# GpSimd in place of VectorE for the two adds of product P1 in the down projection of a one-layer encoder

## The chip, the core and the metric

One core of a Trainium2 chip runs the whole program. TensorE (PE in the rows) multiplies, VectorE (DVE), ScalarE (ACT) and GpSimd (POOL) do the elementwise work, SyncE (SP) issues most DMAs. Each engine takes its own instructions in order and waits on semaphores. The metric is the device time of one execution in microseconds (us), lower is better.

## The reference, cut to what matters

One layer: a forgetting attention and then a dense SwiGLU, each on a normalised residual stream, in float32. S = 512 rows, D = 2048, D_FF = 5632.

```python
h = rmsnorm(x, mix_norm_g[i])
x = x + forgetting_attention(h, fox_w_in[j], ...)
h = rmsnorm(x, ffn_norm_g[i])
x = x + swiglu(h, ffn_w_gate_up[i], ffn_w_down[i])

def swiglu(h, w_gu, w_down):
    gu = jnp.einsum('bsd,df->bsf', h, w_gu)
    gate, up = gu[..., :D_FF], gu[..., D_FF:]
    return jnp.einsum('bsf,fd->bsd', jax.nn.silu(gate) * up, w_down)
```

Only the second product, `w_down`, with the sum into x, is touched here: "down" in what follows.

## The kernel before, in words

**Numbers in two parts.** Each float32 operand is split into a high part (rounded, ScalarE) and a low part (the rest, VectorE), and each product is three matmuls: high by high, high by low, low by high. For a weight tile, `weights_hi` (L1007, L1010, L1014) on ScalarE writes `f_hi`, and `weights_lo` (L1344) on VectorE subtracts it from `f_raw` to get `f_lo`. For the hidden activations, `down_forms_lo` (L1414) does the same on VectorE.

**Seven products in place of eight.** The SwiGLU runs Strassen's scheme in Winograd's form on 2 x 2 blocks. So the work is in units: one unit is one slice of weights with three products (first half of a round, g = 0: P1, P2 and P3) or four (second half, g = 1: P5, P6, P7 and P4). A unit with g = 0 has 18 matmuls of 128 x 512 and one with g = 1 has 24. For g = 1, VectorE first makes sums of the raw weights in place: `sums_t1_t3` (L1350) and `sums_t2_t4` (L1355, L1357); ScalarE and then `weights_lo` follow on these. PE takes a unit when its `f_lo` is done. In PE's rows a unit begins where the output changes from `gemm` to `aux` at L723.

**Rounds.** A round is ROUND_K units with g = 0 and then as many with g = 1. Rounds 0 to 10 are gate and up, rounds 11 to 16 are down: three blocks of 8, 7 and 7 steps, with two rounds each. Around the first round of a block the activations' forms are loaded, so L1414 stands between the weight operations there.

**The results.** In down the results are summed into the tile `rows`, which holds x1, the residual stream. It was stored to DRAM (`dram_x1`, "x_scratch" in the rows) and comes back with four DMAs on SP's queue: `rows[:, 2]` (L390) and `rows[:, 0]` (L393) in round 11, `rows[:, 1]` (L396) and `rows[:, 3]` (L397) right behind the weight loads of the third unit of round 12, that is when PE is done with the last unit but one of round 11. For each of the two column pairs n, GpSimd makes a base of them, an add (L510) and a subtract (L512), when both DMAs of the pair have landed. Even n belongs to rounds 11, 13, 15, odd n to rounds 12, 14, 16.

**At the end of the first half** of a down round r, ScalarE copies the two banks of P1 to `junk_act` (L1027, semaphore `p1_read`), and VectorE adds P2 (L1423, `p2_read`) and P3 (L1428, `p3_read`; in rounds 11 and 12 after GpSimd's base, `base_done`) from PSUM into `rows`. `add_p1`, of which the change is, then adds P1 into two blocks of `rows`: `x1 += P1` (L1436, semaphore `x1_p12`) and `x4 = P1 - x4` (L1437, `x4_p1`), both 128 x 1024 from SBUF to SBUF. VectorE reaches it at unit j = 4 of the second half.

**At the end of the second half**, `down_read` on VectorE waits for `x4_p1` and reads P6 (L1445, `p6_read`) and P7 (L1450 and L1451, `p7_read`) from PSUM, `add_p4` (L1458) reads P4, and at the start of the next round `add_p5` (L1467) and `finish_x4` (L1482) follow. PE may overwrite the banks of P1 in the next round only after `p6_read`. ScalarE's next copy into `junk_act` waits for `x4_p1`.

**Order.** It is written out by hand, per engine, by loops over the units; there is no planner.

Of the kernel before, what the change touches and what calls it, by code (L numbers as in the profile page):

```python
# [30 lines left out]
ALU = mybir.AluOpType  # L31
# [7 lines left out]
def encoder_layer(nc, x, mix_g, ffn_g, w_in, b_f, g_q, g_k, w_out, w_gu, w_down, y):  # L39
# [33 lines left out]
    R_DOWN = NP  # L73
    NR = NP + 2 * len(BLOCKS)
# [20 lines left out]
    with ctx:  # L95
        def at(name, offset, shape, dt=F32):
            return nc.alloc_sbuf_tensor_at(name, shape, dt, offset=offset)

        def sem(name):
            return ctx.enter_context(nc.semaphore(name))  # L100
# [41 lines left out]
        rows = at("rows", AREA_S, [P, ND, NT, CW])  # L142
# [10 lines left out]
        def small(name, shape, dt=F32):  # L153
            n = 4
            for s in shape[1:]:
                n *= s
            offset = place[0]
            place[0] += -(-n // 32) * 32
            assert place[0] <= 229344
            return at(name, offset, shape, dt)  # L160

        junk_act = small("junk_act", [P, 2, CW])
# [24 lines left out]
        def a_lo(k):  # L187
# [47 lines left out]
        p1_read, p2_read, p3_read = sem("p1_read"), sem("p2_read"), sem("p3_read")  # L235
        p6_read, p5_read, p7_read, p4_read = (sem("p6_read"), sem("p5_read"),
                                              sem("p7_read"), sem("p4_read"))
# [8 lines left out]
        x1_p12, x4_p1, x2_p5, x4_p7 = sem("x1_p12"), sem("x4_p1"), sem("x2_p5"), sem("x4_p7")  # L246
# [28 lines left out]
        for b in range(len(BLOCKS)):  # L275
            r = R_DOWN - 1 + 2 * b
# [145 lines left out]
        def _(pool):  # L422
            g = nc.gpsimd
# [83 lines left out]
            for n in range(2):  # L507
                pool.wait_ge(x1_ld[n], 16)
                pool.wait_ge(x1_ld[2 + n], 16)
                g.tensor_tensor(rows[:, n, 2:4], rows[:, n, 2:4], rows[:, 2 + n, 2:4], ALU.add)\  # L510
                    .then_inc(base_done, 1)
                g.tensor_tensor(rows[:, 2 + n, 0:2], rows[:, 2 + n, 0:2], rows[:, 2 + n, 2:4],  # L512
                                ALU.subtract).then_inc(base_done, 1)


        @block.tensor
# [594 lines left out]
        def _(dve):  # L1111
            v = nc.vector
# [23 lines left out]
            def row_sums(n):  # L1136

                dve.wait_ge(ssx_done, NT * ND * (n + 1))
                v.tensor_reduce(ss_sum[:], ss_x[:], AX.X, ALU.add).then_inc(sum_done, 1)
# [148 lines left out]
            def form_sums(q, fa):  # L1288
                dve.wait_ge(xform_read, 2 * q + 2)
                block_sums(q, fa)  # L1290

            def form_lo(q, fa):
                dve.wait_ge(aform_hi, q + 1)
                v.tensor_tensor(a_form[:, q, 1], fa[:, 0:7], f32(a_form[:, q, 0]), ALU.subtract)\
                    .then_inc(aform_lo, 1)
# [45 lines left out]
            def weights_lo(n):  # L1341
                g = UNITS[n][1]
                dve.wait_ge(f_hi_done, HI_COUNT[n])
                v.tensor_tensor(f_lo[:, n % 4, 0:3 + g], f_raw[:, n % 4, 0:3 + g],  # L1344
                                f32(f_hi[:, n % 3, 0:3 + g]), ALU.subtract).then_inc(f_lo_done, 1)

            def sums_t1_t3(n):
                dve.wait_ge(f_ld[n % 4], LANDED[n])
                f = f_raw[:, n % 4]
                v.tensor_tensor(f[:, 0:2], f[:, 0:2], f[:, 1:4:2], ALU.add).then_inc(t_step, 1)  # L1350

            def sums_t2_t4(n):
                f = f_raw[:, n % 4]
                dve.wait_ge(t_step, 3 * T_COUNT[n] + 1)
                v.tensor_tensor(f[:, 3], f[:, 0], f[:, 3], ALU.add).then_inc(t_step, 1)  # L1355
                dve.wait_ge(t_step, 3 * T_COUNT[n] + 2)
                v.tensor_tensor(f[:, 2], f[:, 3], f[:, 2], ALU.add).then_inc(t_step, 1)  # L1357
# [28 lines left out]
            def up_top(r):  # L1386
                for t in range(2):
                    dve.wait_ge(p3_read, 2 * r + t + 1)
                    dve.wait_ge(p5_read, 2 * r + t + 1)
                    v.tensor_tensor(h_top[:, t], h_top[:, t], h_bot[:, t], ALU.add).then_inc(c12_done, 1)  # L1390
# [37 lines left out]
                    v.tensor_tensor(rows[:, 2 + n, t], bank_c[t][:], rows[:, 2 + n, t], ALU.add)\  # L1428
                        .then_inc(p3_read, 1)

            def add_p1(r):
                n = (r - R_DOWN) % 2
                dve.wait_ge(p1_read, 2 * r + 2)
                dve.wait_ge(p2_read, 2 * r + 2)
                x1, x4 = rows[:, n, 0:2], rows[:, 2 + n, 2:4]
                v.tensor_tensor(x1, x1, junk_act[:], ALU.add).then_inc(x1_p12, 1)  # L1436
                v.tensor_tensor(x4, junk_act[:], x4, ALU.subtract).then_inc(x4_p1, 1)  # L1437

            def down_read(r):
                n = (r - R_DOWN) % 2  # L1440
                dve.wait_ge(x4_p1, r - R_DOWN + 1)
                for t in range(2):
                    wait_product(dve, r, True, t)
                    x4 = rows[:, 2 + n, 2 + t]
                    v.tensor_tensor(x4, bank_a[t][:], x4, ALU.add).then_inc(p6_read, 1)  # L1445
                for t in range(2):
                    dve.wait_ge(p6_read, 2 * r + t + 1)
                    wait_product(dve, r, True, 4 + t)
                    x4, x3 = rows[:, 2 + n, 2 + t], rows[:, 2 + n, t]
                    v.tensor_tensor(x4, bank_b[t][:], x4, ALU.add).then_inc(x4_p7, 1)  # L1450
                    v.tensor_tensor(x3, bank_b[t][:], x3, ALU.add).then_inc(p7_read, 1)  # L1451
# [49 lines left out]
            for n in range(NU):  # L1501
                r, g, j = UNITS[n]
                hidden = 1 <= r <= R_DOWN
                last = j == ROUND_K[r] - 1
                sums = n + 2 < NU and UNITS[n + 2][1] == 1
                meeting = (g == 0 and j == ROUND_K[r] - 2) or (g == 1 and j == 0)
                if sums and not meeting:
                    sums_t1_t3(n + 2)
                if n + 1 < NU:
                    weights_lo(n + 1)  # L1510
                if sums and meeting:
                    sums_t1_t3(n + 2)
                if sums:
                    sums_t2_t4(n + 2)
                if g == 0:
                    if r == 0:
                        if j == 1:
                            form_sums(6, fa_a)
                        if j == 2:
                            form_lo(6, fa_a)  # L1520
                            form_sums(7, fa_b)
                        if j == 3:
                            form_lo(7, fa_b)
                            row_sums(1)
                    if hidden:
                        if j == 0:
                            up_top(r - 1)
                        if j == 1:
                            hidden_top(r - 1)
                        if j == 2:  # L1530
                            hidden_bot(r - 1)
                        if j == 3:
                            hidden_sums(r, 0)
                        if j == 5:
                            hidden_sums(r, 1)
                    if r > R_DOWN:
                        if j == 0:
                            add_p5(r - 1)
                            finish_x4(r - 1)
                        if r == NR - 1 and j == 1:  # L1540
                            last_sums(r - 1)
                        if r == NR - 1 and j == 2:
                            last_bottom(r - 1)
                    if last:
                        if r < R_DOWN:
                            read_p2(r)
                        else:
                            add_p2_p3(r)
                else:
                    if r >= R_DOWN and j == 4:  # L1550
                        add_p1(r)
                    if last and r < R_DOWN:
                        second_pass_read(r)
                    if last and r >= R_DOWN:
                        down_read(r)
                        if r < NR - 1:
                            add_p4(r)
                        else:
                            add_p5(r)
                            finish_x4(r)  # L1560
                            last_sums(r)
                            last_bottom(r)
                            add_last_p4(r)
                if n - 4 in LOAD_AT:
                    down_forms_lo(*LOAD_AT[n - 4])
# [24 lines left out]
```

## Time and profile before

| what | us |
|---|---|
| time, median of 3 runs | 2190.46 |
| lowest and highest of the 3 | 2188.57, 2190.71 |
| the profiled execution's own time | 2189.52 |
| its span in the trace | 2187.8 |
| around the span | 1.7 |

In the page PE is busy for 97% of the span, DVE for 70%, ACT for 42%, POOL for 8%. In the 40 slices DVE is at 4 to 5 tenths in the attention and at 7 to 9 tenths from slice 16 on, in the SwiGLU. Down takes about the last fifth of the span. A row of the time line reads: start, duration, engine, line, operation, output<-inputs, shape, count of merged instructions, and in brackets the idle time of the engine ahead of it with what ended it.

### The profile page before, as it was taken

The numbers are of one execution on the slowest core, as the hardware profiler recorded it, in microseconds if no ns is written. First come the engines' busy times: TensorE is split into PE (matmuls) and PEld (weight loads), VectorE is DVE, ScalarE is ACT, GpSimd is POOL, SyncE is SP. The second block draws the span as 40 slices with busy tenths as digits, with TensorE's granted clock in tenths as the row PEclk, the third lists the DMA queues.
The fourth block names the chain that finished last, engine by engine and source line by source line (L and its number), as shares of the span: only waits on it lengthen the run. The fifth ranks groups of instructions, "written<-read, shape, count | busy, mean of one in ns | idle before, by whom it ended". The sixth has DMA issues, their size and how long they took to land.

```text
span 2187.8 us, 27845 instructions
## 1 busy us (share of the span) xinstructions
PE 2129.5 (97%) x10404; PEld 1852.7 (85%) x10404; DVE 1524.6 (70%) x2103; ACT 915.4 (42%) x1225; POOL 183.8 (8%) x356
## 2 busy tenths in 40 slices
PE   9999999999999999999999999999999989999997
PEld 8999999999998887888888888888887777777786
DVE  4544444444464445987888888788798888898888
ACT  5433333333343334444444444444445534444432
POOL 0322213222230000000000000000000001000000
PEclk9999999999999999999999999999999999999999
DMA  6332333333343335566566566567668757757755
GB/s 181 88 92 82 88 85 90 85 89 81 92 144 135 116 106 163 178 226 220 179 222 226 177 219 229 190 207 228 193 207 280 261 201 270 236 177 250 234 175 178
DMA packets 258331, 376.30 MB, mean 172 GB/s; under 512 B 15762, under 2 KB 114100, under 8 KB 257220
## 3 DMA queue, kind: packets, MB, share of 16 engines
q1 hardware_dynamic: 254864, 354.90, 51.6%
q10 hardware_dynamic: 3380, 20.21, 2.2%
q8 instruction: 58, 0.95, 0.2%
q14 instruction: 29, 0.24, 0.0%
HBM read 346.45 MB, written 28.61 MB: 171 GB/s over the span
## 4 chain that ended last, share of the span: by engine, by line
PE 83%; DVE 9%; DMA 6%; issue 1%; SPq 1%; POOL 0%; ACT 0%; DVEq 0%; POOLq 0%; ACTq 0%
PE gemm L522 11%; PE gemm L524 11%; PE gemm L523 11%; PE gemm L723 8%; PE gemm L725 8%; PE gemm L724 8%; PE aux L723 7%; PE aux L725 7%; PE aux L724 6%; DVE f_lo L1344 4%; DMA f_raw<-in_ffn_w_gate_up 3%; DMA f_raw<-in_ffn_w_down 2%; DVE f_raw L1350 2%; PE aux L523 1%; PE aux L524 1%; PE aux L522 1%
## 5 line engine op out<-in xcount | busy, mean ns | idle before, releaser
L1344 DVE TENSOR_TENSOR f_lo<-f_raw,f_hi 128x2048 fp32r<-128x2048 f32 (+1 forms) x264 | 534.2, 2030 | 63.9 <-ACT f_hi L1007 51.4
L522 PE MATMUL gemm<-w_hi,act_t 128*128 128x384 f32 (+2 forms) x1280 | 450.6, 352 | 1.6 <-DVE w_lo L1123 1.6
L524 PE MATMUL gemm<-w_hi,act_t 128*128 128x384 f32 (+2 forms) x1280 | 444.0, 347 | 0.0
L523 PE MATMUL gemm<-w_lo,act_t 128*128 128x384 f32 (+2 forms) x1280 | 443.9, 347 | 0.0
L723 PE MATMUL gemm<-f_hi,a_form 128*128 128x512 f32 x1056 | 412.4, 391 | 0.4 <-DVE rows L1428 0.4
L724 PE MATMUL gemm<-f_lo,a_form 128*128 128x512 f32 x1056 | 411.7, 390 | 0.0
L725 PE MATMUL gemm<-f_hi,a_form 128*128 128x512 f32 x1056 | 411.3, 389 | 0.0
L723 PE MATMUL aux<-f_hi,a_form 128*128 128x512 f32 x792 | 318.3, 402 | 42.8 <-DVE f_lo L1344 42.8
L725 PE MATMUL aux<-f_hi,a_form 128*128 128x512 f32 x792 | 312.2, 394 | 0.0
L724 PE MATMUL aux<-f_lo,a_form 128*128 128x512 f32 x792 | 311.9, 394 | 0.0
L1123 DVE TENSOR_TENSOR w_lo<-w_raw,w_hi 128x768 fp32r<-128x768 f32 (+1 forms) x160 | 160.8, 1009 | 208.5 <-ACT w_hi L818 208.5
L1007 ACT ACTIVATE f_hi<-f_raw 128x1536 fp32r<-128x1536 f32 x132 | 196.0, 1487 | 253.8 <-PE gemm L725 93.2
L522 PEld LDWEIGHTS gemm<-w_hi,act_t 128*128 128x128 f32 x1280 | 241.0, 188 | 12.4 <-issue 2.0
L523 PEld LDWEIGHTS gemm<-w_lo,act_t 128*128 128x128 f32 x1280 | 241.0, 188 | 10.4
L524 PEld LDWEIGHTS gemm<-w_hi,act_t 128*128 128x128 f32 x1280 | 240.8, 188 | 10.1
L723 PEld LDWEIGHTS gemm<-f_hi,a_form 128*128 128x128 f32 x1056 | 199.1, 189 | 42.6 <-DVE rows L1428 0.8
L724 PEld LDWEIGHTS gemm<-f_lo,a_form 128*128 128x128 f32 x1056 | 199.0, 188 | 41.6
L725 PEld LDWEIGHTS gemm<-f_hi,a_form 128*128 128x128 f32 x1056 | 198.8, 188 | 41.7
L1010 ACT ACTIVATE f_hi<-f_raw 128x1024 fp32r<-128x1024 f32 x132 | 139.9, 1060 | 222.2 <-DVE f_raw L1350 218.2
L1014 ACT ACTIVATE f_hi<-f_raw 128x1024 fp32r<-128x1024 f32 x132 | 140.2, 1062 | 210.5 <-DVE f_raw L1357 210.5
L723 PEld LDWEIGHTS aux<-f_hi,a_form 128*128 128x128 f32 x792 | 150.3, 190 | 88.2 <-DVE f_lo L1344 58.5
L818 ACT ACTIVATE w_hi<-w_raw 128x768 fp32r<-128x768 f32 (+1 forms) x160 | 136.4, 883 | 187.8 <-PE gemm L524 187.8
(161 smaller groups left out, 2143.0 us busy)
## 6 DMA issues: line engine op xcount, KB each, us to landing
f_raw<-in_ffn_w_gate_up SPq DMA_DIRECT2D x264, 512.0 KB, 4.2
f_raw<-in_ffn_w_down SPq DMA_DIRECT2D x132, 512.0 KB, 4.8
w_raw<-in_fox_w_in SPq DMA_DIRECT2D x192, 256.0 KB, 3.4
f_raw<-in_ffn_w_gate_up SPq DMA_DIRECT2D x88, 256.0 KB, 4.0
w_raw<-in_fox_w_out SPq DMA_DIRECT2D x16, 1024.0 KB, 5.1
a_raw<-forms_scratch SPq DMA_DIRECT2D x22, 512.0 KB, 6.3
f_raw<-in_ffn_w_down SPq DMA_DIRECT2D x44, 256.0 KB, 4.8
forms_scratch<-fa_a ACTq DMA_DIRECT2D x11, 896.0 KB, 6.3
```

Source lines behind the costliest of these rows:

```text
L522: mm(out, a_hi, b_hi, start=first, stop=False)
L523: mm(out, a_hi, b_lo, start=False, stop=False)
L524: return mm(out, a_lo, b_hi, start=False, stop=last)
L723: mm(banks[t][:], st_hi, hi, start=j == 0, stop=False)
L724: mm(banks[t][:], st_hi, lo, start=False, stop=False)
L725: i = mm(banks[t][:], st_lo, hi, start=False, stop=j == ROUND_K[r] - 1)
L818: a.activation(w_hi[:, j % 2, k, 0:width], w_raw[:, j % 2, k, 0:width], ACT.Copy)\
L1007: a.activation(f_hi[:, n % 3, 0:3], f_raw[:, n % 4, 0:3], ACT.Copy).then_inc(f_hi_done, 1)
L1010: a.activation(f_hi[:, n % 3, 0:2], f_raw[:, n % 4, 0:2], ACT.Copy).then_inc(f_hi_done, 1)
L1014: a.activation(f_hi[:, n % 3, 2:4], f_raw[:, n % 4, 2:4], ACT.Copy).then_inc(f_hi_done, 1)
L1123: v.tensor_tensor(w_lo[:, j % 2, k, 0:width], w_raw[:, j % 2, k, 0:width], f32(w_hi[:, j % 2, k, 0:width]), ALU.subtract).then_inc(w_lo_do ...
L1344: v.tensor_tensor(f_lo[:, n % 4, 0:3 + g], f_raw[:, n % 4, 0:3 + g], f32(f_hi[:, n % 3, 0:3 + g]), ALU.subtract).then_inc(f_lo_done, 1)
```

## The change

The two adds leave VectorE's list and stand at the end of GpSimd's, one pair for each of the six down rounds, with the same semaphores. GpSimd waits for `p1_read` and `p2_read` of the round, does the first add, waits for `p5_read` of the round before (VectorE's last subtract into x4), and does the second.

```diff
@@ gpsimd, behind the two base operations of each n
+            for r in range(R_DOWN, NR):
+                n = (r - R_DOWN) % 2
+                pool.wait_ge(p1_read, 2 * r + 2)
+                pool.wait_ge(p2_read, 2 * r + 2)
+                x1, x4 = rows[:, n, 0:2], rows[:, 2 + n, 2:4]
+                g.tensor_tensor(x1, x1, junk_act[:], ALU.add).then_inc(x1_p12, 1)
+                pool.wait_ge(p5_read, 2 * (r - 1))
+                g.tensor_tensor(x4, junk_act[:], x4, ALU.subtract).then_inc(x4_p1, 1)
@@ vector
-            def add_p1(r):
-                n = (r - R_DOWN) % 2
-                dve.wait_ge(p1_read, 2 * r + 2)
-                dve.wait_ge(p2_read, 2 * r + 2)
-                x1, x4 = rows[:, n, 0:2], rows[:, 2 + n, 2:4]
-                v.tensor_tensor(x1, x1, junk_act[:], ALU.add).then_inc(x1_p12, 1)
-                v.tensor_tensor(x4, junk_act[:], x4, ALU.subtract).then_inc(x4_p1, 1)
@@
                 else:
-                    if r >= R_DOWN and j == 4:
-                        add_p1(r)
                     if last and r < R_DOWN:
```

**GpSimd's list, its end.** Before, the last compute instructions are the two base pairs of n = 0 and n = 1 (the numbers behind the names tell tiles apart):

```order
95 L505 TENSOR_SCALAR rms_neg_98<-rms_x_97 128x4 [waits rms_done]
96 L510 TENSOR_TENSOR rows_82<-rows_82 128x1024 [waits x1_loaded2,x1_loaded0]
97 L512 TENSOR_TENSOR rows_82<-rows_82 128x1024
98 L510 TENSOR_TENSOR rows_82<-rows_82 128x1024 [waits x1_loaded3,x1_loaded1]
99 L512 TENSOR_TENSOR rows_82<-rows_82 128x1024
100 L95 UNCONDITIONAL_BRANCH
```

With the change (L520 and L522 are the two adds of P1; rounds 13 to 16 repeat the last two rows):

```order
96 L510 TENSOR_TENSOR rows_82<-rows_82 128x1024 [waits x1_loaded2,x1_loaded0]
97 L512 TENSOR_TENSOR rows_82<-rows_82 128x1024
98 L510 TENSOR_TENSOR rows_82<-rows_82 128x1024 [waits x1_loaded3,x1_loaded1]
99 L512 TENSOR_TENSOR rows_82<-rows_82 128x1024
100 L520 TENSOR_TENSOR rows_82<-rows_82,junk_act_90 128x1024 [waits p2_read,p1_read]
101 L522 TENSOR_TENSOR rows_82<-junk_act_90,rows_82 128x1024 [waits p5_read]
102 L520 TENSOR_TENSOR rows_82<-rows_82,junk_act_90 128x1024 [waits p2_read,p1_read]
103 L522 TENSOR_TENSOR rows_82<-junk_act_90,rows_82 128x1024 [waits p5_read]
```

The pair of round 11 (100 and 101) stands behind the base of n = 1, which waits for the two loads that are issued in the last unit of round 11.

**VectorE's list, second half of round 11.** Before, from unit j = 4 to the reads of P6 and P7:

```order
1036 L1357 TENSOR_TENSOR f_raw<-f_raw 128x512 [waits t_step]
1037 L1436 TENSOR_TENSOR rows<-rows,junk_act 128x1024 [waits p2_read,p1_read]
1038 L1437 TENSOR_TENSOR rows<-junk_act,rows 128x1024
1039 L1350 TENSOR_TENSOR f_raw<-f_raw 128x1024 [waits f_loaded3]
1040 L1344 TENSOR_TENSOR f_lo<-f_raw,f_hi 128x2048 [waits f_hi_done]
1041 L1355 TENSOR_TENSOR f_raw<-f_raw 128x512 [waits t_step]
1042 L1357 TENSOR_TENSOR f_raw<-f_raw 128x512 [waits t_step]
1043 L1344 TENSOR_TENSOR f_lo<-f_raw,f_hi 128x2048 [waits f_hi_done]
1044 L1344 TENSOR_TENSOR f_lo<-f_raw,f_hi 128x1536 [waits f_hi_done]
1045 L1445 TENSOR_TENSOR rows<-aux,rows 128x512 [waits product_done,x4_p1]
1046 L1445 TENSOR_TENSOR rows<-aux,rows 128x512 [waits product_done]
```

With the change (lines below the edit shift: L1344 is L1353, L1350 is L1359, L1355 and L1357 are L1364 and L1366, L1445 is L1446):

```order
1036 L1366 TENSOR_TENSOR f_raw<-f_raw 128x512 [waits t_step]
1037 L1359 TENSOR_TENSOR f_raw<-f_raw 128x1024 [waits f_loaded3]
1038 L1353 TENSOR_TENSOR f_lo<-f_raw,f_hi 128x2048 [waits f_hi_done]
1039 L1364 TENSOR_TENSOR f_raw<-f_raw 128x512 [waits t_step]
1040 L1366 TENSOR_TENSOR f_raw<-f_raw 128x512 [waits t_step]
1041 L1353 TENSOR_TENSOR f_lo<-f_raw,f_hi 128x2048 [waits f_hi_done]
1042 L1353 TENSOR_TENSOR f_lo<-f_raw,f_hi 128x1536 [waits f_hi_done]
1043 L1446 TENSOR_TENSOR rows<-aux,rows 128x512 [waits product_done,x4_p1]
1044 L1446 TENSOR_TENSOR rows<-aux,rows 128x512 [waits product_done]
```

The two adds are gone from between the weight operations, and the wait for `x4_p1`, once on VectorE's own work, is now one on GpSimd.

## Rows read from the trace of the kernel before

**Rows 1.** The page, part 1: engine, busy us (share), instructions.
```profile
PE 2129.5 (97%) x10404; PEld 1852.7 (85%) x10404; DVE 1524.6 (70%) x2103; ACT 915.4 (42%) x1225; POOL 183.8 (8%) x356
```
**Rows 2.** Waits from 1760 us on: who for whom, total us, times, longest.
```profile
PE aux L723 <- DVE f_lo L1344: 21.3, 20, 3.0
```
**Rows 3.** Time line of POOL: its four operations on `rows`.
```profile
1756.00 2.38 POOL L510 TENSOR_TENSOR rows<-rows 128x1024 f32<-128x1024 f32 x1 [892.01 <-DMA rows<-x_scratch]
1758.34 2.38 POOL L512 TENSOR_TENSOR rows<-rows 128x1024 f32<-128x1024 f32 x1
...
1812.06 3.76 POOL L510 TENSOR_TENSOR rows<-rows 128x1024 f32<-128x1024 f32 x1 [51.34 <-DMA rows<-x_scratch]
1815.78 3.92 POOL L512 TENSOR_TENSOR rows<-rows 128x1024 f32<-128x1024 f32 x1
```
**Rows 4.** Time line of SP's queue, the second load of n = 1.
```profile
1802.09 0.43 SPq L397 DMA_DIRECT2D rows<-x_scratch  x1
```
**Rows 5.** Time line of DVE: end of round 11, start of round 12.
```profile
1801.44 1.30 DVE L1445 TENSOR_TENSOR rows<-aux,rows 128x512 f32<-128x512 f32 x2 [0.16 <-PE aux L725]
...
1807.75 1.75 DVE L1344 TENSOR_TENSOR f_lo<-f_raw,f_hi 128x1536 fp32r<-128x1536 f32 x1
```
**Rows 6.** Time line of PE: start of the second unit of round 12.
```profile
1810.01 0.39 PE L723 MATMUL aux<-f_hi,a_form 128*128 128x512 f32 x1
```
**Rows 7.** Time line of DVE beside POOL's first and third operation.
```profile
1755.95 1.29 DVE L1423 TENSOR_TENSOR rows<-gemm,rows 128x512 f32<-128x512 f32 x2 [0.85 <-DMA rows<-x_scratch]
...
1811.81 1.75 DVE L1344 TENSOR_TENSOR f_lo<-f_raw,f_hi 128x1536 fp32r<-128x1536 f32 x1
```
**Rows 8.** Instructions of `f_lo` from 1815 to 1823 us: ns min/median/max, first and last start.
```profile
L1344 DVE TENSOR_TENSOR f_lo<-f_raw,f_hi x3: 1745/1890/3774, 1815.5 to 1821.2; 128x1536 fp32r<-128x1536 f32 x3
```
**Rows 9.** Time line of DVE in round 12: meeting, third unit, the two adds.
```profile
1843.03 1.28 DVE L1428 TENSOR_TENSOR rows<-gemm,rows 128x512 f32<-128x512 f32 x2
1844.22 2.28 DVE L1344 TENSOR_TENSOR f_lo<-f_raw,f_hi 128x2048 fp32r<-128x2048 f32 x1
...
1851.01 2.29 DVE L1344 TENSOR_TENSOR f_lo<-f_raw,f_hi 128x2048 fp32r<-128x2048 f32 x1
...
1870.12 1.22 DVE L1436 TENSOR_TENSOR rows<-rows,junk_act 128x1024 f32<-128x1024 f32 x1
1871.25 1.22 DVE L1437 TENSOR_TENSOR rows<-junk_act,rows 128x1024 f32<-128x1024 f32 x1
```
**Rows 10.** Time line of PE: starts of units in second halves, round 12.
```profile
1853.35 0.50 PE L723 MATMUL aux<-f_hi,a_form 128*128 128x512 f32 x1
...
1876.73 0.50 PE L723 MATMUL aux<-f_hi,a_form 128*128 128x512 f32 x1 [1.28 <-DVE f_lo L1344]
```
**Rows 11.** Time line of DVE and of PE: third unit of round 13.
```profile
1931.81 2.28 DVE L1344 TENSOR_TENSOR f_lo<-f_raw,f_hi 128x2048 fp32r<-128x2048 f32 x1
...
1935.06 0.39 PE L723 MATMUL aux<-f_hi,a_form 128*128 128x512 f32 x1
```
**Rows 12.** Time line of PE: starts of units in second halves, rounds 14, 15, 16.
```profile
1999.45 0.50 PE L723 MATMUL aux<-f_hi,a_form 128*128 128x512 f32 x1 [1.04 <-DVE f_lo L1344]
...
2029.38 0.50 PE L723 MATMUL aux<-f_hi,a_form 128*128 128x512 f32 x1 [1.18 <-DVE f_lo L1344]
...
2081.06 0.50 PE L723 MATMUL aux<-f_hi,a_form 128*128 128x512 f32 x1 [1.33 <-DVE f_lo L1344]
...
2150.30 0.50 PE L723 MATMUL aux<-f_hi,a_form 128*128 128x512 f32 x1 [0.28 <-DVE f_lo L1344]
```
**Rows 13.** Time line of PE: first units of second halves, rounds 13 and 15.
```profile
1921.17 0.79 PE L723 MATMUL aux<-f_hi,a_form 128*128 128x512 f32 x1 [2.99 <-DVE f_lo L1344]
...
2068.07 0.50 PE L723 MATMUL aux<-f_hi,a_form 128*128 128x512 f32 x1 [2.68 <-DVE f_lo L1344]
```
**Rows 14.** Windows behind these two: busy per engine, PEclk, DMA share, GB/s.
```profile
1921.20:1927.40 6.20, 6.20 (x15) 4.86 (x16) 6.17 (x8) 2.00 (x2) 0.00 (x0) 0.51 0.41 156
...
2068.20:2073.80 5.60, 5.60 (x24) 4.30 (x24) 5.57 (x7) 2.01 (x2) 0.00 (x0) 1.00 0.48 179
```

## The prediction

> **What bounds the kernel now.** I read the page first: PE is busy for 97% of the span and VectorE for 70% [rows 1]. So the change can pay only where PE waits for VectorE. The view of waits from the start of down says how much that is: PE waits for `f_lo` 20 times, 21.3 us in all, 3.0 at most [rows 2]. Most of these waits are at the first unit of a second half, where the weights' DMA comes last and the sums and `f_lo` follow on it; the adds of P1 come later and are not in them. The adds at unit j = 4 can be behind two waits only: 1.28 us in round 12, right behind the adds [rows 10], and 1.18 us in round 14 [rows 12]. The two adds take 1.22 us each and start 1.13 apart, so VectorE is given 2.3 us a round [rows 9], but PE can get back at most 1.28 + 1.18 = 2.5 us of it in the whole of down. (A wait of 0.2 to 0.4 in rounds 11 and 16 is left out.)
>
> Then I looked for what GpSimd does at these moments, and for what stands ahead of the new work in its list. Both speak against the change.
>
> **Part 1: the queue on GpSimd in round 11.** GpSimd works in order, and the pair of round 11 stands behind the base operations of n = 1. These start at 1812.06 in the trace, when their DMA has landed [rows 3]; it was issued at 1802.09 [rows 4]. The issue waits for PE's progress to the last unit of round 11, so nothing in the change brings it forward. VectorE wanted `x4_p1` of round 11 at 1801.44, for its first read of P6 [rows 5]. Before, that was its own finished work; now it waits for GpSimd:
> - One operation of 128 x 1024 with two inputs takes 2.38 us on GpSimd alone, and the next starts 2.34 after it [rows 3]. Four of them, two for the base and two for P1, take 3 x 2.34 + 2.38 = 9.4 us. VectorE stands still then, so nothing disturbs them. They end at 1812.06 + 9.4 = 1821.5.
> - VectorE's read of P6 moves from 1801.4 to 1821.5, by 20 us. Queued behind it are the reads of P7 and P4 and `f_lo` of round 12's second unit. PE needs `p6_read` for the first matmul of round 12 and stands still.
> - From the read on, eight reads of PSUM at about 0.60 us each (two merged ones are 1.28 to 1.30 [rows 5, 9]) take 4.8, and `f_lo` 1.75 [rows 5]. So `f_lo` of the second unit is done at 1821.5 + 4.8 + 1.7 = 1828.0. PE started this unit at 1810.01 [rows 6]. The loss is 18.0 us. Another four such operations (2.4) and the next `f_lo` (1.7) end at 1832.1, just when PE is through the 18 matmuls of the second unit: no more is lost. The weights for these units have long landed meanwhile.
> - Bounds: the landing may be some tenths earlier, since the issue follows PE and less DMA runs beside it; PE may come out of so long a pause at a low clock, which would cost up to 1 us where it isn't hidden by VectorE's reads. 17 to 20 us; I take 17.8.
>
> **Part 2: GpSimd and VectorE side by side, rounds 12 to 16.** Here GpSimd is free when `p2_read` comes, which is the end of L1423. It starts at once, in the most crowded stretch of VectorE, not at j = 4.
> - What the trace shows: L1423, one input from PSUM and one from SBUF, ran its 1.29 us for two beside GpSimd's first operation, and that took 2.38: no disturbance [rows 3, 7]. L1344, both inputs in SBUF, was started at 1811.81, and GpSimd's operation of 1812.06 took 3.76 in place of 2.38 and ended 2.3 after VectorE was done [rows 3, 7]. Then GpSimd's operation of 1815.78 took 3.92, and of three `f_lo` beside it, all of one shape, one took 1.89 and one 3.77 in place of 1.75 [rows 3, 8]. So the two take turns by whole instructions, and VectorE was held for 2.0 us.
> - The sum for a round: GpSimd's first add runs from the end of L1423 for 2.38. For 1.2 of this VectorE does L1428 from PSUM [rows 9], so its next operation, from SBUF, waits for 1.2. The second add goes in behind that operation and holds VectorE for its full 2.38. VectorE has practically no pause there [rows 9]. So it is 2 x 2.38 - 1.2 = 3.56 us late by the third unit of the second half.
> - What PE has in hand at that unit: in round 12 `f_lo` ends at 1851.01 + 2.29 = 1853.30 and PE starts at 1853.35 [rows 9, 10], nothing; in round 13 it ends at 1934.09 and PE starts at 1935.06 [rows 11], 0.9; in rounds 14, 15 and 16 PE already waits for it, by 1.04, 1.33 and 0.28 [rows 12], nothing. So PE loses 3.5 + 2.6 + 3.6 + 3.6 + 3.6 = 16.9.
> - Given back at j = 4: 2.5, as above. The weight loads follow PE, so they absorb nothing. Part 2 is + 14.4 us. Bounds: - 2.5 (no hindrance) to + 17.8 (5 x 3.56, nothing given back).
> - The rule of the Trainium skill that bears on this, in the page SBUF — State Buffer, section Who interferes with whom: a VectorE instruction with two SBUF inputs contends with a GpSimd one that reads SBUF, and whichever issues second blocks fully. By that rule, the trace agrees, with 3.77 in place of 1.75 us; and the sum by it is the one above.
>
> **Part 3: the clock.** After PE's wait of 2.99 us in round 13, 6.2 us passed at a granted clock of 0.51, which is the 1.2 GHz level, and after one of 2.68 us in round 15 the clock stayed at 1.00, the 2.4 GHz level [rows 13, 14]. At the low level half of the time is lost: 3.1 us in the first case, 0 in the other. There are five new or longer waits of 2.6 us or more. At the mean of the two, 1.55, they cost 7.7; some of it is hidden where PE waits again for VectorE two units on. I take 6, with ends 0 and 15.
>
> **The end of the program.** The last stores wait for reads of PSUM long behind the adds, and the store that waits for `x1_p12` is issued earlier. I take nothing for it.
>
> **The sum.** 17.8 + 14.4 + 6 = 38.2 us on the profiled execution's 2189.5, which is 0.9 below the median of the runs: 2227.7, say 2228 us, 1.7% more.
>
> **The rivals.**
> - **Work side by side is free.** Then part 2 is - 2.5 and part 3 nearly nothing, while the queue of round 11 stays: + 17.8 - 2.5 + 0.7 = + 16, 2205.5 us. For it speaks only that L1423 was undisturbed; against it the 3.77 us of an `f_lo` [rows 8]. The Trainium skill's page Perfetto Trace Analysis, section Optimizing Scalar/DVE Operations, says that with a saturated VectorE it may make sense to move work to GpSimd, and warns of the shared port; its first half would be this case. Chance 0.06.
> - **VectorE goes first when its instructions stand back to back.** The rows show GpSimd coming in only behind a pause of VectorE. If the second add has to wait for a real pause, it falls where PE has about 1 us in hand, and VectorE is relieved soon after. Then a round costs 1.2 for the first add and about 0.5 for the second: 5 x 1.7 - 0.9 - 2.5 = + 5. With 17.8 and 2 for the clock, + 25: 2214 us. Chance 0.12.
> - **Not slower: GpSimd is through with round 11's pair before VectorE asks.** The point from which it decides: the load for n = 1 would have to be there 9.4 us before 1801.44, at 1792.0. Then part 1 is 0, and with free side by side the time is 2189.5 - 2.5 = 2187 us. But the load is issued at 1802.09 [rows 4], behind PE's own progress. Chance 0.02.
>
> **How the numbers follow.** Forecast 0.80, rivals 0.06, 0.12, 0.02. The forecast's own ends: 17 + 12.5 + 0 = 29.5 to 19 + 15 + 15 = 49, but both ends at once are unlikely. The range of 8 in 10 takes in the second rival at its lower end, down to 2213 us, and goes to 2240. A difference of 0.2% (4.4 us) is about what a measurement of this kernel can tell from no change. Slower by more: all but the last rival, 0.98. Within 0.2%: 0.01; faster: 0.01.
>
> **What the changed profile would show.** Right, part 1: GpSimd's four operations in a row from about 1812, each near 2.38; L1446 with an idle time of about 20 us released by GpSimd; a PE wait of some 16 us at the start of round 12. Right, part 2: in each of rounds 12 to 16 a weight operation of VectorE longer by 1.2 and one by 2 to 2.4 us behind L1429, and PE waits for `f_lo` of 2.6 to 4.6 us at the second or third unit. Wrong, if the wait for `x4_p1` in round 11 is a few us, if L1353 keeps 2.28 us beside GpSimd's adds, or if VectorE is held but PE has enough in hand. The clock term is right if low stretches follow about half of the new waits.

## The result: 2227.6 us, 1.7% slower

| what | before | with the change |
|---|---|---|
| median, us | 2190.59 (4 runs) | 2227.55 (4 runs) |
| lowest, us | 2188.57 | 2226.65 |
| profiled execution, us | 2189.52 | 2228.3 |
| its span, us | 2187.8 | 2226.5 |

The ratio to before is 1.0169, 95% interval 1.0149 to 1.0189. One of the four executions was disturbed and is left out of the ratio; the other three lie between 2226.65 and 2228.3 us, with a median of 2226.8. The forecast was 2228.

The page of the changed kernel, part 1, answers to [rows 1]; the waits from 1760 us on answer to [rows 2] (who for whom, total us, times, longest). The line numbers below the edit are 9 or 1 higher: `f_lo` is L1353, L1423 is L1432, L1428 is L1437, L1445 is L1446; the two adds are L520 and L522.

```profile
PE 2136.1 (96%) x10404; PEld 1857.4 (83%) x10404; DVE 1526.6 (69%) x2091; ACT 914.9 (41%) x1225; POOL 217.7 (10%) x368
```
```profile
PE aux L732 <- DVE f_lo L1353: 37.3, 19, 4.5
...
DVE rows L1446 <- POOL rows L522: 20.6, 1, 20.6
...
PE aux L732 <- DVE rows L1446: 15.6, 1, 15.6
```

Twelve adds of 1.22 us left VectorE, and it is busy for 2 us more than before (1526.6 against 1524.6): the time that it is held beside GpSimd is counted in its instructions, not as idle time. From 1760 us on, PE's waits for `f_lo` went from 21.3 [rows 2] to 37.3 us, and one new wait of 15.6 us is there.

**Where the 38.7 us came.** I took the starts of PE's units from both time lines, with the same unit side by side:

| start of PE's unit, us | before | changed | difference |
|---|---|---|---|
| round 11, first unit | 1712.25 | 1710.90 | - 1.35 |
| round 11, last unit | 1800.49 | 1797.46 | - 3.03 |
| round 12, second unit | 1810.01 | 1825.27 | + 15.3 |
| round 13, first unit | 1887.77 | 1908.16 | + 20.4 |
| round 14, first unit | 1962.26 | 1985.88 | + 23.6 |
| round 15, first unit | 2034.95 | 2061.78 | + 26.8 |
| round 16, first unit | 2108.39 | 2141.45 | + 33.1 |
| round 16, last unit | 2172.42 | 2211.20 | + 38.8 |

So 18.3 us come between the last unit of round 11 and the second of round 12, and 23.5 us in the five second halves after it. Within these rounds the differences arise in the second halves; from the second unit of round 12 on the first halves run parallel, within 0.02 us each.

**The wait of round 11, seen.** POOL, DVE, PE and SP's queue in the changed kernel, from their time lines:

```profile
1808.60 2.34 POOL L510 TENSOR_TENSOR rows<-rows 128x1024 f32<-128x1024 f32 x1 [49.54 <-DMA rows<-x_scratch]
1810.89 2.34 POOL L512 TENSOR_TENSOR rows<-rows 128x1024 f32<-128x1024 f32 x1
1813.19 2.34 POOL L520 TENSOR_TENSOR rows<-rows,junk_act 128x1024 f32<-128x1024 f32 x1
1815.49 2.34 POOL L522 TENSOR_TENSOR rows<-junk_act,rows 128x1024 f32<-128x1024 f32 x1
...
1817.86 1.29 DVE L1446 TENSOR_TENSOR rows<-aux,rows 128x512 f32<-128x512 f32 x2 [20.61 <-POOL rows L522]
...
1822.65 1.75 DVE L1353 TENSOR_TENSOR f_lo<-f_raw,f_hi 128x1536 fp32r<-128x1536 f32 x1
...
1818.70 0.76 PE L732 MATMUL aux<-f_hi,a_form 128*128 128x512 f32 x1 [15.64 <-DVE rows L1446]
...
1825.27 0.39 PE L732 MATMUL aux<-f_hi,a_form 128*128 128x512 f32 x1
...
1799.06 0.43 SPq L397 DMA_DIRECT2D rows<-x_scratch  x1
```

The load is issued at 1799.06 and lands at 1808.6 (before: 1802.09 and 1812.06 [rows 3, 4]). Then four operations pass without a break, VectorE stands for 20.6 us and PE for 15.6. The eight reads of PSUM take 1817.86 to 1822.65, 4.8 us, as counted, and `f_lo` of the second unit ends at 1822.65 + 1.75 = 1824.40. PE begins this unit only at 1825.27, and its row has no wait. It was still at work on the first unit, at a granted clock of 0.50, which is the 1.2 GHz level, for 4.8 us behind its pause (a window: busy us of PE, PEld, DVE, ACT, POOL, then PEclk, DMA share, GB/s):

```profile
1818.80:1823.60 4.80, 4.80 (x12) 3.73 (x13) 4.80 (x8) 0.00 (x0) 0.00 (x0) 0.50 0.01 2
```

That unit took 6.57 us (1818.70 to 1825.27) in place of 4.08 before.

**Side by side, seen.** DVE and POOL in round 12 of the changed kernel, which answers to [rows 9]:

```profile
1859.00 1.28 DVE L1437 TENSOR_TENSOR rows<-gemm,rows 128x512 f32<-128x512 f32 x2
1860.20 3.56 DVE L1353 TENSOR_TENSOR f_lo<-f_raw,f_hi 128x2048 fp32r<-128x2048 f32 x1
1863.68 3.41 DVE L1359 TENSOR_TENSOR f_raw<-f_raw 128x1024 f32<-128x1024 f32 x1
...
1859.23 2.38 POOL L520 TENSOR_TENSOR rows<-rows,junk_act 128x1024 f32<-128x1024 f32 x1 [41.40 <-DVE rows L1432]
1861.57 4.44 POOL L522 TENSOR_TENSOR rows<-junk_act,rows 128x1024 f32<-128x1024 f32 x1
```

L1437 reads PSUM and keeps its 1.28 for two. `f_lo` takes 3.56 in place of 2.28: it waits 1.28 for L520 to end. Then L522 waits for `f_lo` (4.44 = 2.38 + 2.06), and L1359, next on VectorE, takes 3.41 in place of 1.22: it waits 2.19 for L522. Together 3.47 us; the prediction had 3.56. On GpSimd L522 takes 4.44 or 4.45 in rounds 12, 13, 15 and 16, and 3.06 in round 14. There the operation that it waits for is a short one, the activations' low part (L1414 before, L1423 here), and the one held behind it is `f_lo` of the second unit, with 4.42 us; so in round 14 PE's long wait is at the second unit and not at the third.

### The profile page after: what moved, and what is told of

Its sections match the earlier page's. It is cut to its first block, busy times and chain, and to the rows that moved or that the text cites. A ratio compares the mean times of both kernels' runs of the same rounds, so it can differ in the third digit from the quotient of the medians.

```text
span 2226.5 us, 27845 instructions
## 1 busy us (share of the span) xinstructions
PE 2136.1 (96%) x10404; PEld 1857.4 (83%) x10404; DVE 1526.6 (69%) x2091; ACT 914.9 (41%) x1225; POOL 217.7 (10%) x368
## 4 chain that ended last, share of the span: by engine, by line
PE 83%; DVE 9%; DMA 5%; issue 1%; POOL 1%; SPq 1%; ACT 0%; DVEq 0%; POOLq 0%; ACTq 0%
PE gemm L531 11%; PE gemm L533 11%; PE gemm L532 11%; PE gemm L732 8%; PE gemm L734 8%; PE gemm L733 8%; PE aux L732 7%; PE aux L734 7%; PE aux L733 7%; DVE f_lo L1353 4%; DMA f_raw<-in_ffn_w_gate_up 3%; DVE f_raw L1359 2%; DMA f_raw<-in_ffn_w_down 1%; DMA rows<-x_scratch 1%; PE aux L532 1%; PE aux L533 1%
## 5 line engine op out<-in xcount | busy, mean ns | idle before, releaser
L1353 DVE TENSOR_TENSOR f_lo<-f_raw,f_hi 128x2048 fp32r<-128x2048 f32 (+1 forms) x264 | 539.3, 2049 | 71.6 <-ACT f_hi L1016 55.8
L1359 DVE TENSOR_TENSOR f_raw<-f_raw 128x1024 f32<-128x1024 f32 x132 | 170.0, 1288 | 83.1 <-DMA f_raw<-in_ffn_w_gate_up 48.8
```

## The experiments

Theory: two causes that add up, the queue on GpSimd in round 11 (about 18 us) and the turns that VectorE and GpSimd take in rounds 12 to 16 (some 15 us of waits, and PE's clock behind them). Rivals: all of it is the queue; or all of it is the side-by-side work; or GpSimd's results are simply late. Each kernel ran with the kernel before on the same chip, and the ratios are to those runs: their median was 2191.43 us beside the first four kernels and 2189.94 beside the last three.

### Round 11's pair alone on GpSimd

```diff
+            for r in range(R_DOWN, R_DOWN + 1):
+                ...
-                    if r >= R_DOWN and j == 4:
+                    if r > R_DOWN and j == 4:
                         add_p1(r)
```

> Only round 11's pair is on GpSimd, behind the base of n = 1; rounds 12 to 16 keep their adds on VectorE. Theory (queue): VectorE stands about 20 us for x4_p1, PE some 16 us at the start of round 12, and nothing else moves: 18 us more than before, about 2208.5 us (2206 to 2211). Rival (the whole loss of the change comes from side-by-side work, the long wait being absorbed by later waits for weights): under 5 us more.

Measured: 2208.85 us, ratio 1.0081 (1.0065 to 1.0096), 17.7 us by the ratio. Its waits from 1760 us on:

```profile
PE aux L732 <- DVE f_lo L1353: 21.2, 17, 3.0
...
DVE rows L1454 <- POOL rows L522: 21.0, 1, 21.0
...
PE aux L732 <- DVE rows L1454: 15.8, 1, 15.8
```

The long wait is there with its 21.0 and 15.8 us, and PE's waits for `f_lo` are what they were (21.2 against 21.3 [rows 2]). The queue alone is about 18 us and isn't absorbed later. The rival falls.

### Rounds 12 to 16 alone on GpSimd

```diff
+            for r in range(R_DOWN + 1, NR):
+                ...
-                    if r >= R_DOWN and j == 4:
+                    if r == R_DOWN and j == 4:
                         add_p1(r)
```

> Round 11's pair stays on VectorE, those of rounds 12 to 16 are on GpSimd. Theory (turns by whole instructions): in each of the five second halves one weight operation of VectorE is 1.2 us longer and one 2.2 us, PE waits grow by about 3.2 us a round less what is given back, and low stretches of the clock add some 7 us: 2213 us (2209 to 2217). Rival (work side by side is free, all the loss is the queue): 2188 us.

Measured: 2211.21 us, ratio 1.0089 (1.0072 to 1.0106), 19.5 us by the ratio. Its DVE, POOL and PE in round 12:

```profile
1846.99 3.57 DVE L1353 TENSOR_TENSOR f_lo<-f_raw,f_hi 128x2048 fp32r<-128x2048 f32 x1
1850.48 3.41 DVE L1359 TENSOR_TENSOR f_raw<-f_raw 128x1024 f32<-128x1024 f32 x1
...
1848.37 4.45 POOL L522 TENSOR_TENSOR rows<-junk_act,rows 128x1024 f32<-128x1024 f32 x1
...
1859.61 0.50 PE L732 MATMUL aux<-f_hi,a_form 128*128 128x512 f32 x1 [3.25 <-DVE f_lo L1353]
```

Side-by-side work isn't free. The two halves add up: 0.0081 + 0.0089 = 0.0170, and the change has 0.0169.

### Round 11's pair ahead of the base of n = 1

```diff
             for n in range(2):
                 ...
+                add_p1(R_DOWN + n)
 
-            for r in range(R_DOWN, NR):
+            for r in range(R_DOWN + 2, NR):
```

> All six pairs on GpSimd, but round 11's pair stands ahead of the base of n = 1 in its list. Theory: the wait of 20 us is gone, and round 11 has the same hindrance as the others, 3.5 us at its second unit, where PE waits already: e2's time plus 3 to 5 us, 2217 us (2212 to 2221). Rival (the queue isn't what the long wait hangs on): near 2228 us.

Measured: 2217.15 us, ratio 1.0109 (1.0092 to 1.0125). Its POOL, DVE and PE at the start of round 11's second half (L512 and L514 are the pair here):

```profile
1761.74 2.39 POOL L512 TENSOR_TENSOR rows<-rows,junk_act 128x1024 f32<-128x1024 f32 x1
1764.08 3.32 POOL L514 TENSOR_TENSOR rows<-junk_act,rows 128x1024 f32<-128x1024 f32 x1
...
1763.02 2.18 DVE L1427 TENSOR_TENSOR a_form<-a_raw,a_form 128x1024 fp32r<-128x1024 f32 x1
1765.13 4.42 DVE L1357 TENSOR_TENSOR f_lo<-f_raw,f_hi 128x2048 fp32r<-128x2048 f32 x1
...
1769.60 0.79 PE L736 MATMUL aux<-f_hi,a_form 128*128 128x512 f32 x1 [5.38 <-DVE f_lo L1357]
```

The wait of 20 us is gone with nothing but the order changed. In its place round 11 now pays as the others do: PE's wait at the second unit is 5.38 in place of 2.27 us, which is the 0.97 and 2.14 us by which the two rows of VectorE are longer than the 1.21 and 2.28 of the kernel before. The ratio lies 0.0020 above that of the last kernel (0.0109 - 0.0089), 4.4 us, where 3 to 5 were expected. The two intervals overlap, so it is the rows that show this price, not the two times.

### Both adds beside reads of PSUM

```diff
+            def add_p1_x4(r):
+                ...
+                second = BASE[r] + ROUND_K[r]
+                pool.wait_ge(p1_read, 2 * r + 2)
+                pool.wait_ge(t_step, 3 * T_COUNT[second + 1] + 3)
+                pool.wait_ge(p5_read, 2 * (r - 1))
+                g.tensor_tensor(x4, junk_act[:], x4, ALU.subtract).then_inc(x4_p1, 1)
+            def add_p1_x1(r):
+                ...
+                pool.wait_ge(p2_read, 2 * r + 2)
+                pool.wait_ge(p6_read, 2 * r + 1)
+                g.tensor_tensor(x1, x1, junk_act[:], ALU.add).then_inc(x1_p12, 1)
 ...
+                add_p1_x4(R_DOWN + n)
+                add_p1_x1(R_DOWN + n)
 ...
                     act.wait_ge(x4_p1, r - R_DOWN)
+                    act.wait_ge(x1_p12, r - R_DOWN)
```

The pair of round 11 stands ahead of the base of n = 1 here too. Since the add into x1 comes late, ScalarE's next copy into `junk_act` now waits for it as well.

> Both adds on GpSimd in all rounds, in the right order of its list, but each put beside reads of PSUM on VectorE: the subtract into x4 is let go when VectorE's last weight sum ahead of L1423 is done, the add into x1 when its first read of P6 is done. Theory (only operations with both inputs in SBUF are held): no weight operation of VectorE is longer, and it has 2.3 us a round less to do: 2188 us (2186 to 2190), at most 2.5 us under before. Rival (VectorE is held whatever it reads): about 2 x 2.4 us a round are lost, 10 us or more above before.

Measured: 2191.72 us, ratio 1.0002 (0.9991 to 1.0014), that is between 2.0 us less and 3.1 us more than before: no difference that can be measured. It lies above the 2186 to 2190 us that I expected, so the gain of up to 2.5 us didn't come. Its DVE and POOL in round 12, and at the end the one row of VectorE in round 11 that was held:

```profile
1845.19 1.28 DVE L1446 TENSOR_TENSOR rows<-gemm,rows 128x512 f32<-128x512 f32 x2
1846.39 1.28 DVE L1451 TENSOR_TENSOR rows<-gemm,rows 128x512 f32<-128x512 f32 x2
1847.59 2.39 DVE L1367 TENSOR_TENSOR f_lo<-f_raw,f_hi 128x2048 fp32r<-128x2048 f32 x1
...
1845.41 2.42 POOL L514 TENSOR_TENSOR rows<-junk_act,rows 128x1024 f32<-128x1024 f32 x1 [25.13 <-issue]
1886.43 2.40 POOL L521 TENSOR_TENSOR rows<-rows,junk_act 128x1024 f32<-128x1024 f32 x1 [38.61 <-DVE rows L1460]
...
1763.93 2.18 DVE L1437 TENSOR_TENSOR a_form<-a_raw,a_form 128x1024 fp32r<-128x1024 f32 x1
```

On the same engine the subtract costs 0.11 us where it stands beside the four reads of PSUM at 1845.19 to 1847.67 (`f_lo` behind them takes 2.39 in place of 2.28), and the add beside the reads at the end of the round costs nothing. PE's waits of 1.28 and 1.18 us behind the old place of the adds are gone in its time line, as the prediction had it for j = 4. PE's waits in the second halves of rounds 12 to 16 add up to 13.9 us, 2.6 less than before. So the relief is in the rows, but too small to be seen in the time. Nor is the placing perfect: in round 11 the subtract comes behind the base of n = 0, at 1762.65, and the low part of the activations beside it takes 2.18 in place of 1.21; PE waits 3.24 us there, where it waited 2.27.

### A filler that reads, and one that writes

Both are the kernel before, whose adds stay on VectorE. At the end of L1423 in rounds 12 to 16 GpSimd does work on a spare tile that nobody waits for, each operation behind a wait for the one before.

```diff
+            for r in range(R_DOWN + 1, NR):
+                pool.wait_ge(p2_read, 2 * r + 2)
+                for i in range(4):
+                    ...
+                    g.tensor_tensor(spare[:], spare[:], spare[:], ALU.add).then_inc(spare_step, 1)
```

> The kernel before, with all adds of P1 on VectorE; from round 12 on GpSimd does four filler adds of 128 x 512 on a spare tile of its own, let go at the same moment as the pair in the change (end of L1423). The filler touches nothing that anyone waits for. Theory (VectorE and GpSimd take turns by whole instructions where both inputs of VectorE's are in SBUF): VectorE is held for about 4 x 1.2 less the 1.2 beside L1428, 3.6 us a round, PE loses nearly all of it, nothing is given back, and the clock adds some: 20 to 27 us more, 2211 to 2218 us. Rival (the loss in rounds 12 to 16 comes from the moved work's results being late): 2190.5 us.

```diff
+            for r in range(R_DOWN + 1, NR):
+                pool.wait_ge(p2_read, 2 * r + 2)
+                for i in range(9):
+                    ...
+                    g.memset(spare[:], 0.0).then_inc(spare_step, 1)
```

> As the filler of adds, but nine memsets of 128 x 512 on the spare tile a round, each about 0.53 us, so GpSimd is busy for about as long at the same moments, and writes but reads nothing. Theory (it is GpSimd's reads that contend): no operation of VectorE is longer, 2190.5 us (2188 to 2193). Rival (any access of GpSimd holds VectorE): as the filler of adds, over 2208 us.

Measured: the filler of adds 2207.52 us, ratio 1.0083 (1.0064 to 1.0102); the filler of memsets 2189.98 us, ratio 0.9997 (0.9983 to 1.0010). DVE and POOL in round 12, first beside the adds, then beside the memsets:

```profile
1848.91 2.28 DVE L1353 TENSOR_TENSOR f_lo<-f_raw,f_hi 128x2048 fp32r<-128x2048 f32 x1
1851.11 2.07 DVE L1359 TENSOR_TENSOR f_raw<-f_raw 128x1024 f32<-128x1024 f32 x1
1853.21 1.41 DVE L1364 TENSOR_TENSOR f_raw<-f_raw 128x512 f32<-128x512 f32 x1
1854.66 1.41 DVE L1366 TENSOR_TENSOR f_raw<-f_raw 128x512 f32<-128x512 f32 x1
...
1847.88 7.64 POOL L522 TENSOR_TENSOR spare<-spare 128x512 f32<-128x512 f32 x4 [22.83 <-DVE rows L1432]
```
```profile
1847.38 2.28 DVE L1353 TENSOR_TENSOR f_lo<-f_raw,f_hi 128x2048 fp32r<-128x2048 f32 x1
1849.58 1.22 DVE L1359 TENSOR_TENSOR f_raw<-f_raw 128x1024 f32<-128x1024 f32 x1
1850.84 0.69 DVE L1364 TENSOR_TENSOR f_raw<-f_raw 128x512 f32<-128x512 f32 x1
...
1846.34 5.20 POOL L522 MEMSET spare<- 128x512 f32 x9 [22.48 <-DVE rows L1432]
```

Work whose result nobody needs costs 18 us if it reads SBUF, and nothing that can be measured if it only writes there for 5.2 us at the same moments. So it is GpSimd's reads that cost time there, and neither results that come late nor its being busy as such. In the two traces the way from the first to the last unit of down is 472.8 and 457.1 us long, 15.7 apart; the rest of the difference in time is the part ahead of down. The size was overrated: I expected 20 to 27 us, and 2211 at least, counting 3.6 us a round. The rows show 0.85 + 0.72 + 0.72 = 2.3 us in round 12. Taken one by one, the four adds of POOL's row start at 1847.88, 1849.00, 1852.17 and 1854.15 and take 1.04, 3.09, 1.90 and 1.37 us. So one takes 1.04 us undisturbed and not 1.2; the first passes beside L1437 and ends as `f_lo` begins, the second comes 0.09 us behind the start of `f_lo` and waits for it, and `f_lo` isn't held at all.

### The loads for n = 1 earlier

```diff
-                if n == BASE[R_DOWN] + 18:
+                if n == BASE[R_DOWN] + 12:
```

> The change, with the two loads for n = 1 issued behind the weights of the fifth unit of round 11's second half in place of the third unit of round 12, some 35 us earlier. Theory: they land by about 1785, GpSimd is through with both base and pair before VectorE asks at 1801, and the wait for x4_p1 is gone; but GpSimd's four operations now stand beside weight operations of VectorE in round 11 and hold it, and 2 MB of loads go ahead of weights: 10 to 16 us less than the change, 2212 to 2218 us. Rival (the wait is GpSimd's own slowness, not the landing): still over 2222 us.

Measured: 2219.16 us, ratio 1.0132 (1.0111 to 1.0152); that is 8 us less than the change, where I expected 10 to 16, and outside the 2212 to 2218 us on record. The rival's mark was 2222 us; of the four executions only the profiled one, with 2224.17, lies above it, and its part ahead of down was 6.1 us longer than that of the trace of before. Its POOL, DVE and PE in the second half of round 11:

```profile
1783.73 2.83 POOL L510 TENSOR_TENSOR rows<-rows 128x1024 f32<-128x1024 f32 x1 [15.89 <-DMA rows<-x_scratch]
1786.52 2.84 POOL L512 TENSOR_TENSOR rows<-rows 128x1024 f32<-128x1024 f32 x1
1789.32 2.80 POOL L520 TENSOR_TENSOR rows<-rows,junk_act 128x1024 f32<-128x1024 f32 x1
1792.08 3.33 POOL L522 TENSOR_TENSOR rows<-junk_act,rows 128x1024 f32<-128x1024 f32 x1
...
1784.23 2.88 DVE L1364 TENSOR_TENSOR f_raw<-f_raw 128x512 f32<-128x512 f32 x1
1787.14 2.77 DVE L1366 TENSOR_TENSOR f_raw<-f_raw 128x512 f32<-128x512 f32 x1
1789.83 3.38 DVE L1359 TENSOR_TENSOR f_raw<-f_raw 128x1024 f32<-128x1024 f32 x1
1793.13 4.43 DVE L1353 TENSOR_TENSOR f_lo<-f_raw,f_hi 128x2048 fp32r<-128x2048 f32 x1
...
1797.62 0.80 PE L732 MATMUL aux<-f_hi,a_form 128*128 128x512 f32 x1 [7.52 <-DVE f_lo L1353]
```

The long wait is gone, so it hung on the landing, as said. But four operations of GpSimd now stand against four of VectorE, one each in turn, and every one is held for 2.1 to 2.2 us, the short ones too (L1364: 2.88 in place of 0.69). That is 8.6 us, and PE waits 7.52 of them. The queue's gain is in the rows as counted, and this price I had too low.

## Why the prediction was right, and where its terms were off

**Part 1, the queue of round 11.** Predicted 17.8 us, measured 18.3 (- 3.0 to + 15.3 in the table), and 17.7 by the ratio of the kernel with this part alone. The steps are in the rows: the landing before the four operations, 9.2 us for the four (9.4 predicted), and 4.8 us for the reads. Only the last step came out otherwise. `f_lo` of the second unit was done at 1824.40, which is the sum's 1828.0 less the 3.5 us by which the load landed earlier, but it wasn't what PE waited for: its first unit, at 1.2 GHz behind the pause, ended 0.87 us later. By `f_lo` alone the loss would have been about 17.5 us; the other 0.8 is the clock, the "up to 1 us" of the prediction's bounds. In the kernel with round 11's pair alone that unit took 5.81 us and ended 0.12 us behind `f_lo`. The order of GpSimd's list decided it: changing that alone removed it.

**Part 2, side by side.** The price on VectorE was 3.56 a round in the sum and 3.47 in the rows. In PE's waits of the second halves of rounds 12 to 16 the two time lines have 16.5 us before and 32.7 after (all waits over 0.15 us), so + 16.2, where the sum had 16.9 - 2.5 = 14.4. By rounds: 2.7, 4.0, 1.8, 3.5, 4.3 against 2.2, 2.6, 2.4, 3.6, 3.6. The largest miss is round 13: the 0.9 us in hand were there because PE's first unit ran at the low clock in the trace of before [rows 14]. In the kernel with round 11's pair alone, where it didn't, PE waited 1.30 us at that third unit with the adds still on VectorE. In the changed kernel it didn't either, and PE waited at the second unit too:

```profile
1947.78 0.50 PE L732 MATMUL aux<-f_hi,a_form 128*128 128x512 f32 x1 [1.49 <-DVE f_lo L1353]
...
1957.04 0.79 PE L732 MATMUL aux<-f_hi,a_form 128*128 128x512 f32 x1 [3.52 <-DVE f_lo L1353]
```

What was to be given back at j = 4, 1.28 and 1.18 us, was given back: the waits at these two units are gone. Two readings of the prediction were off without touching its sum: of the 20 waits of [rows 2] only 5 are at the first unit of a second half, with 10.5 of the 21.3 us, not most of them; and the 1.04 us of round 14 [rows 12] are at its second unit, not its third.

**Part 3, the clock.** Predicted 6 us; what is left of the 23.5 us of these halves when the waits' 16.2 are taken off is 7.3. The windows behind three waits (3.26, 2.65 and 2.43 us) in the changed kernel, as in [rows 14] (busy us of PE, PEld, DVE, ACT, POOL, then PEclk):

```profile
1873.00:1878.20 5.20, 5.20 (x13) 4.05 (x14) 5.13 (x6) 2.74 (x3) 0.00 (x0) 0.50 0.59 215
...
2095.00:2101.50 6.50, 5.59 (x24) 4.29 (x24) 6.46 (x7) 2.01 (x2) 4.03 (x2) 1.00 0.42 154
...
2188.90:2192.30 3.40, 3.40 (x9) 2.61 (x8) 3.40 (x4) 2.12 (x2) 0.00 (x0) 0.51 0.33 125
```

The sign that the prediction gave, low stretches behind about half of the new waits, was not met. All five long waits behind the adds (3.26, 3.52, 4.50, 3.52 and 2.43 us, one a round) were followed by a stretch at 1.2 GHz. A unit of a second half takes 5.44 us at full clock; the units behind these five took 1.6 to 2.9 us more, 11.7 in all, where the sum had 3.1 us for half of them. Against that the 3.0 us behind the wait of 2.99 us in round 13 of before [rows 13, 14] fell away; the wait there was 2.00 us now. So the size was near for other reasons than the ones given. Of the two first-unit waits near 2.6 us one was followed by a low stretch (round 12) and one wasn't (round 15), and in the kernel with rounds 12 to 16 alone a wait of 2.47 us in round 16 wasn't. No run holds the clock still, so the size of this term is argued from the rows and not shown by itself. In that kernel the same subtraction leaves 4.7 us, 2.6 less, which is most of the 3.2 us between it and the change in these halves.

**Not foreseen: 3.0 us to the good before anything begins.** The profiled execution of the change is 1.35 us ahead at the start of down, where both kernels are the same, and 1.0 more by the middle of round 11's second half, where its stretches at the low clock were 3.4 us long in all against 9.5; of the 0.7 left, 0.36 is a wait at j = 6 that went with the adds. It hides that parts 2 and 3 together came out 3 us above the forecast. The other profiled executions started down 1.5 to 6.1 us later than before's. And down itself, from its first unit to its last, took 460.2 us in the trace of before but 457.1 in that of the kernel with the memsets, whose other work is the same; one pair of traces can't tell 3 us from nothing. So the hit to 0.5 us is partly luck; a miss of some 3 us was in the terms.

**The rivals.** "Side by side is free" fell with rounds 12 to 16 alone and with the filler. "VectorE goes first back to back" fell with the rows of round 12: L522 came in directly behind `f_lo`, and L1359, which had nothing else to wait for, was held. "Not slower" had its deciding point in the landing; moving the loads showed that the wait goes, and that its place is taken by the same hindrance in round 11.

## What to carry to other kernels

Before work goes to an engine that looks idle, read what stands ahead of it in that engine's list and when that is released: here 4.6 us of work waited behind an operation that stood 49.5 us for a DMA, which the work itself didn't need, and that cost 18 us. Then look at what the engine that is relieved does at that moment: adds of 2.38 us with two inputs in SBUF on GpSimd held VectorE's instructions with two inputs in SBUF by up to 2.2 us each, so that moving 2.3 us of work a round cost it 3.5, while beside reads of PSUM they were all but free. And ask first what the relief can bring: PE waits that end behind the moved work were 2.5 us in all, and a version with the adds beside those reads gained nothing that could be measured.

## What the runs showed of the hardware that I had not expected

- Being held shows as a longer instruction, not as idle time: `f_lo` 3.56 in place of 2.28 with no releaser in its row. A search for idle time would have missed 3.5 us a round.
- Where both engines had work back to back, with the loads moved ahead, they took turns one by one whatever the size: an operation of 0.69 us was 2.88 long beside one of GpSimd, and GpSimd's own rose from 2.38 to 2.8 only. So a series of short operations lost most. Where `f_lo` started 0.09 us ahead of GpSimd's filler add, it kept its 2.28 and the add took 3.09 in place of 1.04.
- Memsets on GpSimd, 5.2 us of them, left VectorE's operations at 2.28, 1.22 and 0.69 us. The Trainium skill says this in SBUF — State Buffer, section Who interferes with whom: an instruction with two SBUF inputs contends with a GpSimd instruction that reads SBUF and not with one that only writes it. The runs agree on both sides: the filler of adds costs 18 us, the filler of memsets nothing that can be measured.
- GpSimd's operation of 128 x 1024 took 2.34 us where VectorE stood still and 2.38 to 2.42 beside its reads of PSUM.
